# The second pair of FFN weight units is multiplied inside the norm, one token half at a time

## The reference

```python
def post_norm(x, y, g, b):
    return layer_norm(ALPHA * x + y, g, b)

def conv_ffn(h, w_up, conv_w, conv_b, w_down):
    u = dwconv3(h @ w_up, conv_w, conv_b)
    g, val = jnp.split(u, 2, axis=-1)
    return (jax.nn.silu(g) * val) @ w_down
...
        xp = post_norm(xp, mod_p[2] * yp, ln_g[i, 0], ln_b[i, 0])
        xs = post_norm(xs, mod_s[2] * ys, ln_g[i, 0], ln_b[i, 0])
        hp = modulate(xp, mod_p[3], mod_p[4])
        hs = modulate(xs, mod_s[3], mod_s[4])
        fp = conv_ffn(hp, ffn_w_up[i], ffn_conv_w[i], ffn_conv_b[i], ffn_w_down[i])
```

## Time and profile before

| | us |
|---|---|
| median of three runs | 1831.74 |
| the profiled execution | 1830.12 |
| its span | 1828.3 |
| TensorE busy | 1728.4 |
| VectorE busy | 1070.4 |
| ScalarE busy | 711.2 |
| GpSimd busy | 644.4 |

### The profile page before, as it was taken

One profiled execution on the slowest core, in us unless ns is written; L12 is line 12 of the kernel. 1 busy time (PEld: TensorE's weight loads), 2 busy tenths in 40 slices (PEclk: granted clock), 3 DMA queues, 4 the chain that ended last, 5 costly groups with the idle time before them and its releaser, 6 DMA issues.

```text
span 1828.3 us, 30131 instructions
## 1 busy us (share of the span) xinstructions
PE 1728.4 (95%) x11412; PEld 1608.8 (88%) x11412; DVE 1070.4 (59%) x1745; ACT 711.2 (39%) x1153; POOL 644.4 (35%) x319
## 2 busy tenths in 40 slices
PE   6899999789999999999998999998889999999996
PEld 3688888678889999999997999997879999999996
DVE  1277776657755614666457545544678781377735
ACT  3255555535432212223246544644363331132324
POOL 3312121236533333333454222222655333233343
PEclk8999999889999999999999999999999999999998
DMA  9722122111355223453211111110212222222221
GB/s 376 266 71 69 54 67 69 34 33 61 116 195 201 82 75 115 151 207 125 80 55 53 47 58 59 47 53 24 70 47 74 75 83 78 69 70 75 87 80 58
DMA packets 55191, 169.42 MB, mean 93 GB/s; under 512 B 7856, under 2 KB 15408, under 8 KB 55088
## 3 DMA queue, kind: packets, MB, share of 16 engines
q1 hardware_dynamic: 48752, 163.79, 26.1%
q10 hardware_dynamic: 6336, 4.20, 0.7%
HBM read 159.04 MB, written 4.72 MB: 90 GB/s over the span
## 4 chain that ended last, share of the span: by engine, by line
PE 70%; DVE 8%; POOL 7%; issue 5%; ACT 5%; DVEq 3%; DMA 2%; ACTq 1%; SPq 0%; POOLq 0%
PE pj L635 58%; POOL wlo L519 4%; DMA awr<-in_w_ada 2%; PE mO L1065 2%; PE psO L846 2%; PE psS L811 1%; PE pfrow L660 1%; POOL ss L533 1%; PE psT L827 1%; DVE pr L2054 1%; ACT pr L1393 1%; ACTq L1266 1%; POOL X L572 1%; DVE sm L2039 1%; PE mS L1021 1%
## 5 line engine op out<-in xcount | busy, mean ns | idle before, releaser
L481 POOL TENSOR_TENSOR wlo<-wraw,whi 128x1024 fp32r<-128x1024 f32 (+1 forms) x124 | 320.5, 2585 | 814.0 <-ACT whi L1211 814.0
L635 PE MATMUL pj<-Hh,whi 128*128 128x320 f32 x2368 | 568.6, 319 | 22.5 <-ACT Hh L1756 4.2
L635 PE MATMUL pj<-Hl,whi 128*128 128x320 f32 x2368 | 548.9, 311 | 3.0 <-POOL Hl L504 2.0
L635 PE MATMUL pj<-Hh,wlo 128*128 128x320 f32 x2368 | 550.7, 311 | 0.0
L635 PEld LDWEIGHTS pj<-Hh,whi 128*128 128x128 f32 x2368 | 397.8, 190 | 53.6 <-issue 37.0
L635 PEld LDWEIGHTS pj<-Hl,whi 128*128 128x128 f32 x2368 | 401.2, 190 | 4.6 <-POOL Hl L504 3.1
L635 PEld LDWEIGHTS pj<-Hh,wlo 128*128 128x128 f32 x2368 | 402.3, 190 | 0.3
L1211 ACT CAST whi<-wraw 128x1024 fp32r<-128x1024 f32 (+1 forms) x175 | 194.2, 1110 | 281.5 <-PE pj L635 241.2
L1959 DVE SCALAR_TENSOR_TENSOR fcv<-fus,vec,fcv 128x127 f32<-128x127 f32 (+1 forms) x176 | 229.1, 1343 | 15.1 <-issue 15.1
L1837 DVE SCALAR_TENSOR_TENSOR X<-pj,mods,X 128x128 f32<-128x128 f32 (+5 forms) x120 | 45.4, 434 | 219.5 <-PE pj L635 219.3
L635 PE MATMUL pj<-Gh,whi 128*128 128x320 f32 x704 | 168.8, 311 | 0.8 <-POOL wlo L519 0.8
(11 more groups left out here) (311 smaller groups left out, 2173.0 us busy)
## 6 DMA issues: line engine op xcount, KB each, us to landing
wraw<-in_w_up SPq DMA_DIRECT2D x88, 512.0 KB, 3.5
fwr<-in_w_ada SPq DMA_DIRECT2D x56, 512.0 KB, 5.9
wraw<-in_w_dn SPq DMA_DIRECT2D x32, 704.0 KB, 4.1
awr<-in_w_ada SPq DMA_DIRECT2D x40, 512.0 KB, 10.9
wraw<-in_w_qkv SPq DMA_DIRECT2D x24, 512.0 KB, 3.5
wraw<-in_w_mlin SPq DMA_DIRECT2D x24, 512.0 KB, 3.4
sx<-h32t SPq DMA_DIRECT2D x128, 32.0 KB, 2.0
wraw<-in_w_wo SPq DMA_DIRECT2D x8, 512.0 KB, 3.5
```

The source lines that it names most:

```text
L481: nc.gpsimd.tensor_tensor(wlo[k][:, 0:width], wraw[k][:, 0:width], whi[k][:, 0:width].bitcast(F32), ALU.subtract).then_inc(w_lo, 1)
L635: last = mm(out[:, c, 0:HALF], w, x[:, j, c * HALF:(c + 1) * HALF], start=(j == 0 and n == 0), stop=(j == n_k - 1 and n == 2))
```

## The change

In the two norms ahead of an FFN (n = 0 and 2) TensorE gets more to do. After the first half of pair 0, `norm_pair` multiplies the first half of pair 1 in whole units, and after the second half of pair 0 the second half of pair 1. Pair 1 goes into `st_mu` (k = 0) and `st_va` (k = 1), whose halves are free once the statistics of that half have been read. It has weights of its own, `wcr`, `wch` and `wcl`, which lie where `Gl` will be: SyncE loads them during the output projection, VectorE splits them there, behind tiles 2 and 3 of `gated`. The ordinary `wraw`, `whi`, `wlo` then skip pair 1, and all counts behind it are 2 lower (`away`). The unit that VectorE splits behind the norm is now the first of pair 2 instead of the first of pair 1. ScalarE copies pair 1 out of `st_mu` and `st_va`. The full-width `up(1)` of the first FFN half is gone. The diff, cut to its core (the counts that only subtract `2 * away[0]` are left out):

```diff
+            with ExitStack() as g:
+                wcr = [sb(f"wcr{k}", [P, D], F32, g) for k in range(2)]
+                wch = [sb(f"wch{k}", [P, D], F32R, g) for k in range(2)]
+                wcl = [sb(f"wcl{k}", [P, D], F32R, g) for k in range(2)]
             Gl = sb("Gl", [P, GH, TP], F32R, s)
...
+            def load_away(layer):
+
+                for k in range(2):
+                    sp.dma_start(wcr[k][:, :], a["w_up"][4 * layer * GH + 2 + k]).then_inc(wc_landed[k], 16)
...
-            load_run(a["w_wo"], U_WO + 2, KT - 2, D, at=2)
+            load_pair(a["w_wo"], U_WO + 2, 0, D, 2)
+            sp.wait_ge(o_full, 2 * DA_HEADS)
+            load_away(0)
+            load_run(a["w_wo"], U_WO + 4, KT - 4, D, at=4)
...
-            load_run(a["w_mlout"], U_MLOUT, KT, D)
+            load_run(a["w_mlout"], U_MLOUT, 4, D)
+            sp.wait_ge(mo_full, 3 * ML_HEADS)
+            sp.wait_ge(c_out, 32 * ML_HEADS)
+            load_away(1)
+            load_run(a["w_mlout"], U_MLOUT + 4, KT - 4, D, at=4)
...
                         if i == 0 and j == 3:
                             square_stats(n, 1)
+                    for k in range(2):
+                        tile(pair + 1, k, FULL, read=(), spare=(wch[k], wcl[k]), weights=(wc_lo, n + k + 1), halves=(c,),
+                             done=tile_done if i else None, out=(st_mu, st_va)[k])
+                away[0] += 1
...
                     if half == 0:
                         norm_pair(b // 2, n)
-                        up(1)
...
-                    def body(i, width=D):
-                        if half == 0 and isinstance(i, int) and i == 0:
-                            act.wait_ge(w_hi, b + 3)
+                    def body(i, width=D, norm=None):
+                        if norm == 0:
+                            act.wait_ge(w_hi, b + 5 - 2 * away[0])
...
-                        evac(b // 2 + i, 0, fus[0][:, :], pairs=2)
-                        if half or not isinstance(i, int) or i > 0:
+                        evac(b // 2 + i, 0, fus[0][:, :], pairs=2, src=st_mu if norm else None)
+                        if norm is None:
                             split(b // 2 + i + 1, 0, width)
-                        evac(b // 2 + i, 1, fus[1][:, :], pairs=2)
-                        split(b // 2 + i + 1, 1, width)
+                        evac(b // 2 + i, 1, fus[1][:, :], pairs=2, src=st_va if norm else None)
+                        if norm is None:
+                            split(b // 2 + i + 1, 1, width)
+                        elif norm == 0:
+                            split(b // 2 + 2, 1, free=b)
...
+            def split_away(layer, k):
+
+                dve.wait_ge(wc_landed[k], 16 * (layer + 1))
+                ts(wch[k][:, :], wcr[k][:, :], 1.0, None, ALU.mult)
+                dve.drain()
+                tt(wcl[k][:, :], wcr[k][:, :], wch[k][:, :].bitcast(F32), ALU.subtract).then_inc(wc_lo, 1)
...
                     tt(sx[:, 0:TP], sx[:, 0:TP], X[:, j, :], ALU.add)
                     dve.drain()
+                    if base in (U_WO, U_MLOUT) and j in (2, 3):
+                        split_away(int(base == U_MLOUT), j - 2)
...
-            layer_norm(0, U_WO, 2 * KT, third=U_FFN0 + 2)
+            layer_norm(0, U_WO, 2 * KT, third=U_FFN0 + 4)
```

More of the change, by code:

```diff
@@ L306, in hybrid_step @@
         w_hi, w_lo = sem("w_hi"), sem("w_lo")
+        wc_landed, wc_lo = [sem(f"wc_landed{k}") for k in range(2)], sem("wc_lo")
         mlast_done = sem("mlast_done")
@@ L365, in _ @@
             sp.dma_start(ident[:, :], a["mats"][:, 0]).then_inc(const_in, 16)
+            away = [0]
             def load(src, pair, k, width, first=False):
                 if not first:
[L370 removed]
+                    sp.wait_ge(w_lo, 2 * pair + (k - 1 - 2 * away[0]))
                 sp.dma_start(wraw[k][:, 0:width], src).then_inc(w_landed[k], 16)
@@ L435, in load_ffn @@
                     at = (2 * layer + half) * 2 * GH
-                    if layer:
+                    if half == 0:
+                        load_pair(a["w_up"], b, 0, D, at)
+                        away[0] += 1
+                    if layer and half:
                         load_run(a["w_up"], b, 2 * GH, D, at=at)
+                    elif layer:
+                        load_run(a["w_up"], b + 4, 2 * GH - 4, D, at=at + 4)
                     else:
-                        for i in range(3):
+                        for i in range(3) if half else (2,):
                             load_pair(a["w_up"], b, i, D, at)
@@ L489, in split_ffn @@
                     if j == 0:
-                        pool.wait_ge(w_lo, base + first + 1)
+                        pool.wait_ge(w_lo, base + first + 1 - 2 * away[0])
                     else:
@@ L579, in _ @@
             h_lo(0)
-            split_ffn(U_FFN0, 1, 2)
+            away[0] += 1
+            split_ffn(U_FFN0, 1, 4)
             add_half(1, 0)
@@ L583, in _ @@
             h_lo(1)
-            pool.wait_ge(w_lo, U_MLIN + 2)
+            pool.wait_ge(w_lo, U_MLIN + 2 - 2 * away[0])
             for j in range(KT):
@@ L595, in _ @@
             h_lo(2)
-            split_ffn(U_FFN1, 3, 2)
+            away[0] += 1
+            split_ffn(U_FFN1, 3, 4)
             add_half(3, 0)
@@ L960, in project_rest @@
                 tile(v, 0, range(CUT), pairs=2, read=(pj_added, added + 3), weights=(part_lo, n + 1))
-                tile(v, 0, range(CUT, KT), pairs=2, weights=(w_lo, base + 3))
+                tile(v, 0, range(CUT, KT), pairs=2, weights=(w_lo, base + 3 - 2 * away[0]))
                 tile(v, 1, FULL, pairs=2, read=(pj_added, added + 4))
@@ L1204, in _, with split, evac @@
             fn = nc.scalar.activation
-            def split(pair, k, width=D, guard=True):
-                act.wait_ge(w_landed[k], 16 * (pair + 1))
+            away = [0]
+            def split(pair, k, width=D, guard=True, free=None):
+                act.wait_ge(w_landed[k], 16 * (pair + (1 - away[0])))
                 if guard:
-                    act.wait_ge(tile_done, 2 * pair + k - 1)
+                    act.wait_ge(tile_done, 2 * pair + k - 1 if free is None else free)
                 nc.scalar.copy(whi[k][:, 0:width], wraw[k][:, 0:width]).then_inc(w_hi, 1)
-            def evac(pair, k, dst, pairs=1):
+            def evac(pair, k, dst, pairs=1, src=None):
                 act.wait_ge(tile_done, 2 * pair + k + 1)
-                nc.scalar.copy(dst.rearrange("p (a b) -> p a b", a=2), pj[k if pairs == 2 else 0][:, :, 0:HALF]
-                               ).then_inc(pj_copied, 1)
+                src = pj[k if pairs == 2 else 0] if src is None else src
+                nc.scalar.copy(dst.rearrange("p (a b) -> p a b", a=2), src[:, :, 0:HALF]).then_inc(pj_copied, 1)
             def split_spare(base, k):
-                act.wait_ge(w_landed[k], 16 * (base // 2 + 1))
+                act.wait_ge(w_landed[k], 16 * (base // 2 + 1 - away[0]))
                 nc.scalar.copy(wnh[k][:, :], wraw[k][:, 0:D]).then_inc(w_hi, 1)
@@ L1351, in body @@
                         nc.scalar.copy(g, fpr[:, :]).then_inc(g_hi, 1)
-                    body(0)
-                    with act.Fori(1, GH - 1) as i:
+                    body(0, norm=None if half else 0)
+                    if half == 0:
+                        body(1, norm=1)
+                    with act.Fori(1 if half else 2, GH - 1) as i:
                         body(i)
```

26 lines of the change are left out of this document (15 added, 11 removed).

## The result

The changed kernel takes 1834.97 us, the median of 14 runs (1832.34 to 1838.64), and the kernel before, in its own 14 runs, 1829.99 us (1826.42 to 1832.53). The measured ratio is 1.003, with a 95% interval of 1.0021 to 1.0038: 5.0 us slower by the medians, 3.8 to 7.0 by the interval.

The account below looks back on a forecast made before the run. TensorE, busy 1728.4 of 1828.3 us, was taken as the bound. Pair 2's later start (0.7 + 0.55) and half clock (1.5 + 1.5) sum to 4.2 us slower: 1831.7 + 4.2 = 1835.9 us, range 1829 to 1839.5.

Parts of the forecast that it names:

- The chain: Pair 0's copies to pair 2's start, held by the count for pair 1's copy: 11.6 us; 0.7 and 0.55 us later.
- What is won ahead of it: Up to pair 1's end, inserted matmuls fill TensorE's idle time: 3.8 us won in layer 0, 4.0 in layer 1.
- The clock: Half clock behind the new wait ahead of pair 2: 1.5 us lost for each layer, bounds 0 and 3.0.
- the sum of 4.2 us: Whole kernel slower by 0.7 + 0.55 + 1.5 + 1.5 = 4.2 us.
- same: Whole kernel's time within 0.2% (3.7 us) of the kernel before: chance 0.37.
- slower: Whole kernel slower by more than 0.2% (3.7 us): chance 0.49.
- Side parts: VectorE's extra splits and SyncE's extra loads in the output projections: cost taken as 0.
- The bound of 3.4 us a layer: Upper bound in the projection if GpSimd rows hold back both instructions of each VectorE split, making tile 4 late.
- A: Rival: pair 2 starts as soon as pair 1 ends, no wait; 7.8 us won, 1823.9 us; 8 in 100.
- B: Rival: GpSimd's remainder misses the first convolution, 1.9 us less in each layer; 1832.1 us; 10 in 100.
- C: Rival: no fall of the clock behind the wait ahead of pair 2; 1.25 us slower, 1833.0 us; 14 in 100.
- D: Rival: VectorE's splits in the projection reach TensorE; 11.0 us slower, 1842.7 us; 6 in 100.

Follow-up runs that it names:

- the loosened guard: Changed kernel, but pair 2 of the first FFN half waits for pair 0's copies, no longer pair 1's: 1827.3 us, ratio 0.9984 to before.
- the untouched guard with the move: Changed kernel, guard kept, with 18 inserted matmuls of pair 1 moved into the 2.65 us wait ahead of tile 6: 1827.68 us, ratio 0.9987.
- the filling: Changed kernel plus 29 matmuls with unread result in each norm, run during the wait ahead of pair 2: 1832.53 us, ratio 1.001 to before.
- the run of the side parts: Kernel before plus only the change's extra SyncE loads and VectorE splits, their result unused: 1829.72 us, ratio 0.9998.
- half filling: Changed kernel plus 14 matmuls with unread result in each norm, ahead of pair 2: 1832.33 us, ratio 1.0015 to before.

## Why the prediction was right

**The chain.** Right in place, cause and length: 11.6 us from pair 0's copies to pair 2 were forecast, and 468.61 to 480.18 is 11.57, 1363.04 to 1374.52 is 11.48; the forecast waits of 4.55 and 4.6 us are 4.47 and 4.40. That the count and not the data holds pair 2 is shown by the loosened guard, that the chain moves with pair 0 by the untouched guard with the move.

**What is won ahead of it.** The 3.8 us up to the end of pair 1 were there: with 4.0 us in layer 1 they make 7.8, less the 1.3 us of waiting left there 6.5. Once the guard no longer took them back, and pair 3 had its weights, the kernel was 5.3 us faster by the medians and 7.0 by the ratio. The profile shows the taking back too: counted from the first wait for `Hh` in the norm, pair 2 starts 0.9 us later than before in layer 0 (480.18 - 440.21 against 482.01 - 442.98) and 0.7 us later in layer 1, 1.7 us in all, where 0.7 + 0.55 = 1.25 were forecast.

**The clock.** The fall was forecast and came in both layers, and the filling shows that it costs time. Its size was off: the term "1.5 us for each layer" measured 2.5, inside its bounds of 0 and 3.0. It had been read from one wait of one profiled execution, the 4.19 us near layer 1's output projection, behind which the clock was back after 3.4 us. The change doesn't touch that wait, and it is as long in the changed kernel, yet there the half clock lasted from 1281.0 to 1287.8:

```profile
1282.19 0.90 PE L664 MATMUL pj<-Hh,whi 128*128 128x320 f32 x2 [4.19 <-ACT Hh L1797]
...
1282.19:1287.60 5.41, 5.41 (x20) 0.50 0.00 0
```

The second row is TensorE alone behind it: 20 matmuls, where 37 would fit. Over all nine profiled kernels the same wait was followed by about 3.4 us of half clock twice and by 6.8 us seven times. The forecast had read the rarer and cheaper of two outcomes as the price of this length. With two prices of 1.5 and 2.5 us and one wait read, that the sum of 4.2 us came within 0.8 us of the measured 5.0 is in part luck.

By the profiled executions the sum is 1.7 + 2 x 2.5 = 6.7 us. That agrees with the traces: from the first wait for `Hh` in the norm to the second copy of pair 2, layer 0 took 53.4 us before and takes 56.8 now, layer 1 53.5 and 56.65, 6.6 us in all. The runs say 5.0 (3.8 to 7.0). The profiled spans differ by only 2.8 us, because the profiled execution of the changed kernel was 2.8 us ahead when it reached the first norm (440.21 against 442.98 us for the same wait), and gained another 1.1 us between the two stretches. Of the first 2.8 us, 1.4 arose inside layer 0's output projection, where before the clock was at 1.2 GHz from 396.1 to 399.5 behind a wait of 1.88 us, while the changed kernel kept the full clock behind the same wait of 1.90 us; all 2.8 us were there at 402.4, ahead of the first new split. So a single profiled span says little about a change of this size.

**The absolute time.** The forecast of 1835.9 us stood on the 1831.74 us of three runs, while 14 runs of the kernel before gave 1829.99. It was 1.75 us too high in its base and 0.8 us too low in its step (4.2 for 5.0), and the first made up for the second. The chances for "same" and "slower" also don't add up from the parts named: 22 + 14 + 7 = 43 in 100 and 40 + 6 = 46 in 100, where 0.37 and 0.49 are written. The forecast of slower doesn't hang on it.

**Side parts.** 0 was taken, and 0.9998 (0.9988 to 1.0007) was measured for them alone. The bound of 3.4 us a layer assumed that a GpSimd row stands in the way of both instructions of a split. In the traces one met the first only, which took 1.2 us longer. The 2.53 us for a split by itself were too much, since the 1.80 in them was a stretched row too; the two instructions need 0.73 + 1.23 us.

**The rivals.** A did not happen by itself, for the reason given against it. B did not either: the third tap of the first convolution, beside GpSimd's remainder (from 470.92), took 2.91 us, as before. C is out by the windows at 0.50. D is out by the run of the side parts.

```profile
471.48 2.91 DVE L2012 SCALAR_TENSOR_TENSOR fcv<-fus,vec,fcv 128x127 f32<-128x127 f32 x2 [0.17 <-issue]
```

## What to carry to other kernels

A guard that counts copies in program order also holds work whose buffer is free. When work moves to another buffer, ask of each count behind it which buffer it protects; here one changed count turns 0.3% slower into 0.2% faster. Work that is put into idle time ahead of a fixed chain only moves the idle time behind it, unless the start of the next work is taken off the chain too. And of the idle times in one stretch, the single wait of 2.65 us, which also brought the half clock, was the better place for new work: 18 matmuls moved there won some 3.3 us a layer, nearly as much as the 3.8 to 4.0 us that the change wins with 48 ahead of the guard.

A price read from one wait of one profiled execution can be off by a factor of two without anything being changed. Look for the same wait in the profiles of the other kernels before taking it as the price.

## What the runs showed of the hardware

Two things had not been expected. The half clock behind a wait is not one price for a length. Counted over the nine profiled kernels, in steps of 0.2 us, for these waits, which stand apart from other long ones:

| wait of TensorE | full clock kept | half clock for some 3.4 us | for some 6.8 us |
|---|---|---|---|
| 2.3 to 2.4 us, ahead of pair 3 (guard loosened) and pair 2 (half filling) | 2 | 1 | 0 |
| 2.35 us, near 976 us, outside the change | 0 | 7 | 2 |
| 2.48 us, near 960 us, outside the change | 6 | 3 | 0 |
| 2.65 us, in the first half of the norms | 0 | 13 | 1 |
| 4.19 us, near 1282 us, outside the change | 0 | 2 | 7 |
| 4.4 to 4.5 us, ahead of pair 2 | 0 | 0 | 4 |

The same wait in code that no edit touched comes out differently from one profiled execution to the next, and 2.48 us kept the full clock more often than 2.35 us. The two longest waits had the longer stretch in 11 of 13 cases, the shorter ones in 3 of 35; what decides a single case, these runs don't show.

And VectorE's cast of 128x1024 next to GpSimd's `ss` took 1.91 us instead of 0.73, as if it started only when GpSimd's row had ended (408.07, then some 0.6 us to 408.62).
